# Context slots set one by one inside the conditioning blocks of a hybrid retention / GLA layer

## The reference

```
mod   = silu(c) @ w_mod + b_mod                        # (12288,)
sh1, sc1, g1, sh2, sc2, g2 = split(mod, 6)
mod_c = silu(c_ctx) @ w_mod[:, :4096] + b_mod[:4096]   # shc, scc
h  = rms_norm(x,   norm_mix_pre) * (1 + sc1) + sh1
hc = rms_norm(ctx, norm_mix_pre) * (1 + scc) + shc
p  = h  @ w_in                                         # 11296 columns
pc = hc @ w_in[:, :3616]
y  = retention and gated linear attention on p, pc, merged, @ w_out
h_state = x + g1 * rms_norm(y, norm_mix_post)
h_state += g2 * rms_norm(swiglu(norm(h_state) ...), norm_ffn_post)
```

## Time and profile before

| | |
|---|---|
| device time, median of 3 runs | 1828.54 us (1825.78 to 1828.55) |
| device time of the profiled execution | 1829.82 us |
| span of the profiled execution | 1828.1 us |
| TensorE busy | 1778.0 us, 97% |
| VectorE, ScalarE, GpSimd busy | 58%, 43%, 11% |
| mean granted TensorE clock | 0.985 |
| opening (start of the span to the last context slot) | 0 to 173.4 us |

### The profile page before, as it was taken

The page is one execution under the profiler, slowest core; times in us unless marked ns, Lnnn a source line. Parts: engine busy times, 40 slices in busy tenths (PEclk is TensorE's granted clock), DMA queues, the critical chain, the costliest instruction groups (busy, mean ns, idle before and its releaser), DMA issues.

```text
span 1828.1 us, 22057 instructions
## 1 busy us (share of the span) xinstructions
PE 1778.0 (97%) x8012; PEld 1430.6 (78%) x8012; DVE 1052.1 (58%) x1076; ACT 788.5 (43%) x861; POOL 200.0 (11%) x201
## 2 busy tenths in 40 slices
PE   5889999999999999999999999999999999999997
PEld 2446888888778888888888898888888888888886
DVE  5777666564765766766665545545454444444444
ACT  6664222222644544544544445444444444343442
POOL 1431000000005723540000000000000000000000
PEclk9899999999999999999999989999999999999998
DMA  8879988886988865754778636666666666766652
GB/s 313 302 253 332 321 316 308 308 305 236 325 303 305 280 194 172 225 172 152 247 224 322 200 121 196 185 191 188 193 187 191 188 191 187 259 189 193 191 191 78
DMA packets 182285, 422.14 MB, mean 231 GB/s; under 512 B 12816, under 2 KB 13120, under 8 KB 171600
## 3 DMA queue, kind: packets, MB, share of 16 engines
q1 hardware_dynamic: 156288, 304.14, 52.7%
q10 hardware_dynamic: 17856, 82.43, 12.3%
q0 software_dynamic: 8080, 34.75, 5.6%
HBM read 397.66 MB, written 23.61 MB: 230 GB/s over the span
## 4 chain that ended last, share of the span: by engine, by line
PE 91%; DVE 3%; ACT 3%; issue 2%; DMA 1%; POOL 1%; ACTq 0%; DVEq 0%; POOLq 0%
PE ps L1350 27%; PE ps L1338 27%; PE ps L1342 27%; PE ps L1395 2%; DVE w_lo L927 2%; ACT w_hi L591 2%; PE ps L1472 1%; PE ps L1565 1%; PE ps L1581 1%; PE ps L1619 1%; PE ps L1662 1%; DMA wm<-in_w_mod 1%; PE ps L1369 0%; POOL xr_t L358 0%; DMA rows<-in_b_mod 0%
## 5 line engine op out<-in xcount | busy, mean ns | idle before, releaser
L927 DVE TENSOR_TENSOR w_lo<-raw,w_hi 128x1024 fp32r<-128x1024 f32 x568 | 712.5, 1265 | 563.2 <-ACT w_hi L591 560.9
L591 ACT ACTIVATE w_hi<-raw 128x1024 fp32r<-128x1024 f32 x568 | 597.5, 1060 | 876.6 <-PE ps L1350 848.1
L1338 PE MATMUL ps<-w_hi,h_hi 128*128 128x512 f32 x1536 | 485.2, 397 | 0.0
L1342 PE MATMUL ps<-w_hi,h_lo 128*128 128x512 f32 x1536 | 475.4, 391 | 0.0
L1350 PE MATMUL ps<-w_lo,h_hi 128*128 128x512 f32 x1536 | 421.8, 390 | 0.5 <-DVE w_lo L927 0.5
L1342 PEld LDWEIGHTS ps<-w_hi,h_lo 128*128 128x128 f32 x1536 | 288.9, 188 | 62.1
L1350 PEld LDWEIGHTS ps<-w_lo,h_hi 128*128 128x128 f32 x1536 | 288.6, 188 | 61.9 <-DVE w_lo L927 0.9
L1338 PEld LDWEIGHTS ps<-w_hi,h_hi 128*128 128x128 f32 x1536 | 285.5, 188 | 59.5 <-issue 1.9
L939 DVE SCALAR_TENSOR_TENSOR acc<-wm,csil,acc 128x2048 f32<-128x2048 f32 (+1 forms) x60 | 141.0, 2351 | 102.6 <-DMA wm<-in_w_mod 102.6
L1342 PE MATMUL ps<-w_hi,hid_lo 128*128 128x512 f32 x352 | 109.4, 392 | 0.0
L1338 PE MATMUL ps<-w_hi,hid_hi 128*128 128x512 f32 x352 | 109.0, 391 | 0.0
(11 more groups left out here) (257 smaller groups left out, 1311.9 us busy)
## 6 DMA issues: line engine op xcount, KB each, us to landing
raw<-in_w_in SPq DMA_DIRECT2D x176, 512.0 KB, 5.4
wm<-in_w_mod ACTq DMA_DIRECT2D x64, 1024.0 KB, 7.0
raw<-in_ffn_w_gate SPq DMA_DIRECT2D x88, 512.0 KB, 4.5
raw<-in_ffn_w_up SPq DMA_DIRECT2D x88, 512.0 KB, 4.4
raw<-in_ffn_w_down SPq DMA_DIRECT2D x88, 512.0 KB, 4.8
raw<-in_w_mod SPq DMA_DIRECT2D x64, 512.0 KB, 5.2
raw<-in_w_out SPq DMA_DIRECT2D x32, 512.0 KB, 5.0
px<-stage ACTq DMA_DIRECT2D x44, 256.0 KB, 6.6
```

The source lines that it names most:

```text
L591: act.activation(w_hi[:, j % SPLIT, :, :], raw[:, j % RAW, :, :], ACT.Copy).then_inc(w_high, 1)
L927: dve.tensor_tensor(w_lo[:, j % SPLIT, :, :], raw[:, j % RAW, :, :], w_hi[:, j % SPLIT, :, :].bitcast(F32), ALU.subtract).then_inc(w_low, 1)
L1338: pe.matmul(o, hi[:, kk, c], w_hi[:, q, e, :], start=kk == 0, stop=False)
L1342: pe.matmul(o, lo[:, kk, c], w_hi[:, q, e, :], start=False, stop=False)
```

## The change

The eight context slots of the opening are placed otherwise. Blocks 0 to 2 stay. Each of the blocks 3 to 7 has one context slot between its fourth and its fifth slot; (2,1), (3,0) and (3,1) stand behind block 7. The context slots are then at 28, 37, 46, 55, 64, 69, 70 and 71 (before: 32, 33, 50, 51, 68, 69, 70, 71). `mod_end` becomes 7, 15, 23, 32, 41, 50, 59, 68 (before: 7, 15, 23, 31, 41, 49, 59, 67), and `H1_AT` becomes 20, 37, 55, so the hand-placed work of ScalarE and VectorE shifts with them. `take_mod_columns` of blocks 3 and 5 moves out of the context slots to behind slot `mod_end[n] + 2` (34 and 52), and that of block 7 moves from context (2,0) to context (2,1), slot 69. No instruction is added or left out.

```diff
         opening = []
         for n in range(MOD_BLOCKS):
-            opening += [("mod", n, j) for j in range(8)]
-            opening += [("ctx", (n - 3) // 2, e) for e in range(2)] if n in (3, 5, 7) else []
-        opening += [("ctx", QUARTERS - 1, e) for e in range(2)]
+            opening += [("mod", n, j) for j in range(4)]
+            opening += [("ctx", (n - 3) // 2, (n - 3) % 2)] if n >= 3 else []
+            opening += [("mod", n, j) for j in range(4, 8)]
+        opening += [("ctx", 2, 1)] + [("ctx", QUARTERS - 1, e) for e in range(2)]
         mod_end = [opening.index(("mod", n, 7)) for n in range(MOD_BLOCKS)]
...
-                    take_n = 2 * n + 3 if n < QUARTERS - 1 and j == 0 else None
                     products(s, 0, 4 * n + 2 * j, KT - 1, CTX, 0,
-                             between=(lambda t=take_n: take_mod_columns(t)) if take_n is not None else None)
+                             between=(lambda: take_mod_columns(MOD_BLOCKS - 1)) if (n, j) == (2, 1) else None)
...
-                if s - 2 in mod_end and mod_end.index(s - 2) in (0, 1, 2, 4, 6):
+                if s - 2 in mod_end[:-1]:
                     take_mod_columns(mod_end.index(s - 2))
```

## The result

The changed kernel takes 1830.05 us (median of 20 runs, 1826.26 to 1835.25), the kernel before 1826.19 us in the runs beside it (20 runs, 1824.42 to 1829.28). The ratio is 1.0021, with a 95% interval of 1.0013 to 1.0029: slower by 3.8 us, or by 2.4 to 5.3. The predicted +2.1 us has the sign right and lies just outside that interval. The absolute figures, 1830.6 us forecast and 1830.05 measured, agree by luck: the forecast stood on 1828.54 us, the median of three runs, and twenty runs of the same kernel give 1826.19. The profiled execution of the changed kernel has a span of 1830.8 us and took 1832.47 us.

What follows compares the result with a forecast made beforehand. TensorE bounds the kernel, and in the opening VectorE's rate during GpSimd's low parts binds. The terms 0.0 - 2.4 + 2.9 + 1.6 sum to +2.1 us, 1830.6 us against the median 1828.54; 8-in-10 range 1825.5 to 1834.

Steps and rivals of the forecast that it cites:

- What bounds the kernel: Whole kernel: TensorE is busy for 97% of the span, so the opening's gain or loss reaches the end one for one.
- Part 1: Stretch from slot 28 to slot 37: both orders reach slot 38 at the same time, gain 0.0.
- Part 2: The two GpSimd stretches: one more split gets past VectorE ahead of GpSimd, -1.2 us each.
- Part 3: Tail: TensorE stands 3.35 us before slot 70, conditioning slots come 0.5 us faster; together +2.9 us.
- Part 4: Tail: one short stretch at the low clock behind the standstill, +1.6 us.
- the counterexample of the earlier trace: Stretch 33.5 to 37.0 us, 1.94 of 3.50 us busy, kept full clock; by it the tail may pay no clock loss.
- The sum: All terms together: 0.0 - 2.4 + 2.9 + 1.6 = +2.1 us.
- the forecast's own: Range of the forecast itself, without rivals: 1828.5 to 1832.5 us, chance 0.55.
- rival C: Middle gains nothing, as GpSimd's low parts only move with high_pair; the tail leaves +4.5 us, 1833.0 us; chance 0.15.
- The sign that I had set for C: Trace after: slot 64 starting after 145 us would show the slower case, against the forecast 143 to 144.
- Rival B: Intended effect in full: ScalarE and VectorE no longer idle behind a pair, at most -13.1 us, 1820 us; chance 0.08.
- Rival A: Middle loses its low clock after slots 41 to 43 and 59 to 61: 4.3 us back, 1826.3 us; chance 0.15.

Runs made afterwards that it cites:

- experiment 5: Kernel before, with GpSimd's low parts of quarters 1 and 2 computed for 16 of 256 columns, the rest zero: 1818.52 us, ratio 0.9955.
- experiment 2: Middle of the kernel before with the tail of the changed kernel: 1832.31 us, ratio 1.0019 to the kernel before.
- experiment 3: Kernel before, with only the columns of block 7 taken one context slot later (69 instead of 68): 1834.61 us, ratio 1.0032.
- experiment 1: Middle of the changed kernel with the tail of before, measured twice: 1825.81 and 1827.25 us, ratios 0.9994 and 1.0004 to the kernel before.
- experiment 4: Changed kernel with 12 unread matmuls between slots 69 and 70: 1829.58 us, ratio 1.0016 to the kernel before.
- fill: 12 unread matmuls between slots 69 and 70 of the changed kernel: 1829.58 us; with GpSimd's low parts also cut: 1823.21 us.
- experiment 6: GpSimd's low parts cut to 16 of 256 columns: in the changed kernel 1823.63 us (0.9983), in changed middle with tail of before 1820.65 us (0.9957).
- experiment 9: Kernel before, low parts of quarters 1 and 2 on VectorE instead of GpSimd, with high_pair under the context slot pair: 1817.27 us, ratio 0.9942.
- experiment 10: Changed middle, tail of before, low parts on VectorE and high_pair in the wait for the single context slot: 1817.43 us, ratio 0.9948.

## Why the prediction was right, and where it was off

**What bounds the kernel**: right. The changed kernel's span behind slot 72 is 1653.8 us, before 1654.7: the opening is handed on nearly one for one. From one execution to the next this rest is not fixed, though: over all the profiles it lies between 1652.7 and 1658.8 us.

**Part 1**, slot 28 to slot 38 without a difference: right, 20.44 against 20.63 us, with `modulate` hidden under the high products of slot 37.

**Part 2**, "-1.2 us each": this is the term that failed. The mechanism behind it, GpSimd slowing VectorE's splits and TensorE waiting for them, is shown by the cut of experiment 5 (-8.2 us). One more split does get past VectorE ahead of GpSimd, and slot 43 is earlier. But I stopped the count there: TensorE still waits, at slots 44 and 45, and in all as long as before (6.9 us against 6.4). In time the middle is the mean of 0.9994 and 1.0004, and, with the contention cut, 0.9957 against 0.9955: nothing shown, instead of -2.4.

The profiles show where the first reading went wrong. From slot 28 to slot 64 both orders do the same work. It takes 69.70, 68.33 and 69.10 us with the middle of before (the kernel before, experiments 2 and 3), and 67.44, 67.47, 67.41 and 67.47 us with the changed one (the changed kernel, experiment 1 twice, experiment 4): 1.6 us less on the mean. The pair that I compared, 69.70 with 67.44, is nearly the most favourable of all. And slot 64 is not a fair end, for in the changed order the low clock reaches into it. Counted to slot 68, the middle's gain is 1.0 to 2.1 us with the tail of before (73.90 and 72.85 us against 71.81 and 71.76), and between -0.1 and 0.6 with the changed tail (76.69 against 76.76 and 76.14), where slot 64 is a context slot. Why the timed runs do not show even the 1 to 2 us of experiment 1's profiles stays open.

**Part 3**, the tail, +2.9: right. Standstill 3.35 forecast, 3.19 to 3.20 shown as a wait in all four profiles with late columns and no fill (10.08 us from slot 69's start to slot 70's, against 6.71 before from slot 68's start, which holds the columns, to slot 69's: 3.4). The conditioning slots behind slot 64 take 3.71 us instead of 4.20, the 0.5 of the forecast. Its reason, that they follow a context slot, is not shown: in experiment 3, which leaves them in their old place, four of them take 3.75 us (slots 64 to 67).

**Part 4**, the clock behind the standstill, +1.6: right in kind every time, and in size mostly. Slot 70 takes 7.19, 7.21 and 7.25 us in experiments 3, 2 and 6 (1.6 to 1.7 lost) and 8.24 in the changed kernel (2.7). The fill takes it away in both profiles. In time it is worth 0.9 and 1.5 us, not told from 0. All four profiles with a standstill and no fill went to half clock behind it, and the two filled ones did not; the counterexample of the earlier trace rows did not carry over. The Trainium skill ("TensorE: Matmul & The Clock Gate", section "HAM oscillation"), by which such gaps put the engine back to half clock, agrees with these traces.

**The sum**: with part 2 at nothing, 0.0 + 0.0 + 2.9 + 1.6 = +4.5, inside the measured 2.4 to 5.3 and near the 3.8. The measured +3.8 lies in the stated range, which is -3.0 to +5.5 counted from 1828.54 us, and just in the forecast's own, 0.0 to +4.0. The point, +2.1, was 1.7 us low, and the middle's term is what made it so. The arithmetic is rival C's, and so in the main is the reason: what TensorE waits for in the GpSimd stretches did not shrink. Only the splits themselves are slowed a little less (the five beside GpSimd in the first stretch take 8.9 us, before 9.9). The sign that I had set for C, slot 64 after 145 us, did not show it: slot 64 came at 142.92. Rival B is excluded by experiments 1 and 6. Rival A's price was real: the low clock of the middle went in experiments 5 and 9, with the contention, and this change did not remove it.

## What to carry to other kernels

An engine's idle time behind a long piece of work is not a cost until the bound engine is seen to wait for it; here the spread slots gave nothing that the timing shows, and the idle time turned out to be a good place for work that stood elsewhere (experiments 9 and 10). When a wait seems to shrink, add up the waits to the end of the disturbance, not to one slot in it. When slots are reordered, look for the last result that a late slot needs and count what lies between the two: the change took 5.55 us of cover from a chain of 5.2 us. And when a term is about a microsecond, compare several profiles of the same order before it goes into a sum.

## What the runs showed of the hardware

- While GpSimd subtracts two SBUF tiles (128x512), VectorE's subtraction of two SBUF tiles (128x1024) takes 2.02 us on the mean of five, instead of 1.22. GpSimd is slowed as well: its subtraction takes 2.27 us beside the splits, and 1.29 us at 98.37 us in the changed kernel, where VectorE is idle for most of it. Its four `scale_pair` operations (128x256) take 2.40 us before, at 86 us, where VectorE does not split beside them, and 4.50 us in the changed kernel, where it does.
- The same kernel scatters by some us. The kernel before lies between 1824.05 and 1830.13 us in its runs, and the changed one between 1826.26 and 1835.25. With the contention cut and no standstill, five runs lie between 1817.96 and 1819.45 (experiment 5), but six of the other order between 1815.52 and 1821.61 (experiment 6), so the low clock of the opening is not shown to be the cause of the scatter.
- A single standstill of 3.2 us between dense matmuls was followed by the 1.2 GHz level in all four profiles that had one unfilled. Twelve matmuls (2.96 us) in it kept the 2.4 GHz level in both profiles that had them.
